# Two decoder layers written out without loop or barrier, the first eight expert blocks fixed by the program, a loop for second blocks alone

## The chip, the cores and the metric

The kernel runs on one core of one Trainium2 chip. The metric is the device time of one execution in microseconds, the median of several runs. The core has five instruction streams that run side by side and meet only at semaphores: PE (TensorE, matmuls and transposes), DVE (VectorE), ACT (ScalarE), POOL (GpSimd) and SP (SyncE, which issues the DMAs).

## The reference, cut to what matters

```python
for i in range(DEPTH):                     # DEPTH = 2, 256 tokens, D_MODEL = 1024, float32
    h = rms_norm(x, mix_norm_g[i])
    proj = h @ w_in[i]                     # SSD, gMLP, attention and gate columns
    ...                                    # three branches
    merged = g_ssd * (y_ssd @ w_br_ssd[i]) + g_sgu * (y_sgu @ w_br_sgu[i]) + g_mla * (y_mla @ w_br_mla[i])
    x = x + merged @ w_out[i]
    h = rms_norm(x, ffn_norm_g[i])
    if i % 2 == 0: x = x + swiglu(h, ...)          # dense, 2816 wide
    else:          x = x + moe_ffn(h, ...)         # 8 experts, 3584 wide, top 2 of 8
```

`moe_ffn` weighs each expert's output by a softmax over the token's two largest router logits; an expert that a token did not choose has weight zero for it.

## The kernel before, in words

**Exact products.** Every large weight panel (512 columns, 2 MB) comes in by DMA and is cut into four pieces of 128x1024. ACT copies a piece to a rounded "high" part (`w_hi`, in the mixer `mixer_hi`), DVE subtracts to get the "low" part (`w_lo`), and PE does three matmuls for each product: high by high, low by high, high by low. PE waits for each piece on `lo_made`. `w_hi` has six slots (`HI_SLOTS`), DVE and ACT work up to four pieces ahead (`AHEAD`).

**Two layers in one loop.** Each engine runs `Fori(0, DEPTH)`: the mixer (branches, `out` projection), then the norm and transposes of the feed-forward part, then, under `If(L < 1)`, the dense feed-forward. At the end of an iteration each of PE, ACT and DVE adds one to `arrived`; POOL waits for three, fills the padding of the convolution with zeros, clears the semaphores and adds one to `go`, on which all start again through `begin`. This is the barrier of the text below.

**The router and the items.** After layer 1 and its barrier, PE computes the logits (L1113), DVE chooses two experts for each token, and PE ranks the tokens of each expert (to L1122). DVE then builds a table of items (L1992 to L2026): an item is one block of at most 128 tokens of one expert, so there are eight items, and one more for each expert with over 128 tokens (at most 11 in all, `MAX_ITEMS`). The number of items goes to `item_tab` and signals `routed`.

**The items.** PE gathers an item's tokens with a one-hot `pick` matrix (L1130), DVE and ACT make `xg_hi` and `xg_lo`. A barrier follows. The item is 21 panels (gate, up and down of seven column ranges). At its first up panel PE scatters the output of the item before (L1142, from `ysb` by way of `wpickT`) and DVE adds it to `x` (L2051); for the first item this output is zeros (L2057). At its last up panel PE gathers the next item's tokens. Items 0 to 6 (`STRAIGHT` = 7) are written out. The rest are a loop `Fori(STRAIGHT, n_items)` with a barrier ahead of each iteration. After the loop comes one more barrier, the scatter of the last item and the output DMA (L713). SP's own loop over items is `Fori(0, n_items)`; it reads the expert's number from `item_tab` and keeps a ring of seven slots (`MOE_RING`) filled ahead of use, over the end of an item too.

Of the kernel before, what the change touches and what calls it, by code (L numbers as in the profile page):

```python
# [12 lines left out]
P = 128  # L30
# [205 lines left out]
STRAIGHT = EXPERTS - 1  # L236
assert len(MOE.pieces) % HI_SLOTS == 0 and EARLY <= MOE.first[1]
SCATTER_BANKS = (6, 7, 1, 3)

# [19 lines left out]
def hybrid_trunk(nc, A, out):  # L259
    with ExitStack() as ctx:  # L260
# [180 lines left out]
        ring_full = [sem(f"ring_full{s}") for s in range(MOE_RING)]  # L441
        ring_used = [sem(f"ring_used{s}") for s in range(MOE_RING)]
# [5 lines left out]
        fills_begun = sem("fills_begun")  # L448
        routed = sem("routed")
        finished = sem("finished")  # L450

# [4 lines left out]
        def local(name):  # L456
# [3 lines left out]

        bank_full = local("bank_full")
        bank_free = [local(f"bank_free{b}") for b in range(8)]
        act_steps = local("act_steps")
# [8 lines left out]
            "kpe_made", "kv_copied", "gated", "hsq_made", "hmean_made", "hroot_made", "hnorm_made", "max_made",  # L472
# [4 lines left out]
            "picked", "gathered", "xg_made", "xg_hi_made", "xg_lo_made", "wpickT_full", "wpickT_made",  # L477
            "y_copied", "scattered", "added", "zeroed",
            "logits", "chosen", "ranks", "gap_made", "gap_exp",
            "zeros_made")}  # L480
# [5 lines left out]
        splitters = {}  # L486

# [11 lines left out]
        def piece_free(eng, c):  # L499

            if c >= MIXER_HI_SLOTS:
                what, n = USED[c - MIXER_HI_SLOTS]
                if what == "job":
                    eng.wait_ge(bank_full, JOB[n] + 1)
                else:
                    eng.wait_ge(S["mixer_piece_used"], n)
# [15 lines left out]
        def take(eng, name):  # L522

            keep_ahead(eng, name)
            eng.wait_ge(bank_full, JOB[name] + 1)
            return ps[:, JOB[name] % 8]
# [5 lines left out]
        def given(eng, name):  # L532

            keep_ahead(eng, name)
            eng.wait_ge(bank_free[JOB[name] % 8], JOB[name] // 8 + 1)

        def wait_panel(eng, split, kind, i, past=0):

            eng.wait_ge(S["panel_done"], past * len(split.order) + split.at[(kind, i)] + 1)
# [14 lines left out]
        def hidden_free(eng, split, i, tiles, past=0):  # L554

            if i > 2 - tiles:
                wait_panel(eng, split, "down", i - (1 if tiles == 2 else 2), past)
# [7 lines left out]
        def hi_free(eng, split, c, past=0):  # L565

            c += past * len(split.pieces)
            if c >= HI_SLOTS:
# [3 lines left out]
                if last:  # L572
                    eng.wait_ge(S["panel_done"], u + 1)
                else:
                    eng.wait_ge(S["piece_used"], c - HI_SLOTS + 1 - u)
# [5 lines left out]
        def begin(eng, turn):  # L581

            eng.wait_ge(go, turn)
            eng.sem_inc(begun, 1)
# [25 lines left out]
        def _(sp):  # L610
# [4 lines left out]
            with sp.Fori(0, DEPTH) as L:  # L615
                one = bass.ds(L, 1)

                def panel(use):
# [5 lines left out]
                    if c == 0:  # L624

                        sp.sem_inc(fills_begun, 1)
# [11 lines left out]
                sp.sem_inc(fills_begun, 1)  # L638
# [14 lines left out]
                sp.wait_ge(go, L + 1)  # L653
# [7 lines left out]
                with sp.If(L < 1):  # L661
# [17 lines left out]
            def moe_panel(item, u, expert):  # L679
                kind, p = MOE.order[u]  # L680
                c, width = MOE_PANELS[p]
                s, n = u % MOE_RING, u // MOE_RING

                sp.wait_ge(ring_used[s], item * ITEM_USES + (uses0[s] + n + 1))
# [9 lines left out]
            for u in range(RING):  # L694
                moe_panel(0, u, slice(0, 1))

            sp.wait_ge(go, DEPTH + 1)
            for u in range(RING, MOE_RING):
                moe_panel(0, u, slice(0, 1))
# [3 lines left out]
            with sp.Fori(0, n_items) as i:  # L703
                e = sp.value_load(item_tab[0:1, bass.ds(i, 1)], min_val=0, max_val=EXPERTS - 1)
                for u in range(MOE_RING, len(MOE.order)):
                    moe_panel(i, u, bass.ds(e, 1))
                with sp.If(i < n_items - 1):
                    e2 = sp.value_load(item_tab[0:1, bass.ds(i + 1, 1)], min_val=0, max_val=EXPERTS - 1)
                    for u in range(MOE_RING):
                        moe_panel(i + 1, u, bass.ds(e2, 1))  # L710
# [7 lines left out]
        def _(pool):  # L718
# [8 lines left out]
            pool.sem_inc(go, 1)  # L727
            with pool.Fori(0, DEPTH):
                pool.wait_ge(arrived, 3)

                pool.memset(xin[:, :, :, 0:TAPS - 1], 0.0).then_inc(S["zeros_made"], 1)
                pool.wait_ge(S["zeros_made"], 1)
                pool.sem_clear(cleared)
                pool.sem_inc(go, 1)
            pool.wait_ge(arrived, 3)
            n_items = pool.value_load(item_tab[0:1, ITEM_SLOTS:ITEM_SLOTS + 1], min_val=EXPERTS, max_val=MAX_ITEMS)
            pool.sem_clear(cleared)  # L737
            pool.sem_inc(go, 1)
            pool.wait_ge(arrived, 3)
            pool.sem_clear(cleared)  # L740
            pool.sem_inc(go, STRAIGHT)
            with pool.Fori(STRAIGHT, n_items):
# [6 lines left out]
        def _(pe):  # L749
# [3 lines left out]
            def bank(name):  # L753
# [4 lines left out]
                if i >= 8:  # L758
                    pe.wait_ge(bank_free[i % 8], i // 8)
# [30 lines left out]
            def ffn(split, tiles, slot_of, lhs, acc, before_turn=None, before_down=None, early=0, past=0):  # L790
# [4 lines left out]
                panels_past, pieces_past = past * len(split.order), past * len(split.pieces)  # L795

                def turn_hidden(i):
                    pe.wait_ge(S["h_made"], past * n_panels + i + 1)
# [5 lines left out]
                for c, (u, at_, n, ends) in enumerate(split.pieces):  # L804
                    kind, i = split.order[u]
                    s, width = slot_of(u), split.widths[i]
                    if kind == "up" and i and at_ == 0:
                        pe.wait_ge(S["hid_made"], past * n_panels + i)
                    if kind == "down" and at_ == 0:
                        pe.wait_ge(S["hid_made"], past * n_panels + i + 1)  # L810
                    if pieces_past + c >= early:
                        pe.wait_ge(S["lo_made"], pieces_past + c + 1 - early)
# [23 lines left out]
                    if ends:  # L836
                        unreleased.append((s, S["panel_done"], panels_past + u + 1))
# [13 lines left out]
            with pe.Fori(0, DEPTH) as L:  # L851
# [15 lines left out]
                def split_piece():  # L867
# [3 lines left out]
                    pe.wait_ge(S["mixer_lo_made"], c + 1)  # L871
                    return mixer_piece(c)[2:]

                def project(name, lhs):
# [19 lines left out]
                    unreleased.append((s, bank_full, turn[0]))  # L894

                def close_part(br, i, y, ready):
# [8 lines left out]
                    if i == 2:  # L905
                        pe.wait_ge(S["yT_lo_made"], 4 * ("ssd", "sgu", "mla").index(br) + 4)
# [3 lines left out]
                begin(pe, L + 1)  # L910
# [3 lines left out]
                for t in range(NT):  # L914
                    pe.wait_ge(S["normed"], t + 1)
                    for hh in range(2):
                        turn_over(f"ht{t}{hh}", [xn[:, t, c * P:(c + 1) * P] for c in range(4 * hh, 4 * hh + 4)])
                pe.wait_ge(S["h_lo_made"], 4)

                for n in range(3):  # L920
# [14 lines left out]
                    unreleased.append((s, bank_full, turn[0]))  # L935
# [4 lines left out]
                pe.wait_ge(S["adt_made"], 1)  # L940
# [8 lines left out]
                pe.wait_ge(S["silu_made"], 6)  # L949
# [12 lines left out]
                for t in range(NT):  # L962
                    pe.wait_ge(S["lat_normed"], t + 1)
# [11 lines left out]
                unreleased.append((s, bank_full, turn[0]))  # L975
# [7 lines left out]
                unreleased.append((s, bank_full, turn[0]))  # L983
                project("u1", hsplit)

                pe.wait_ge(S["xd_made"], 1)
# [6 lines left out]
                for c in range(NT):  # L993
# [10 lines left out]
                    pe.wait_ge(S["xs_made"], c + 1)  # L1004
                    for g in range(2):
                        pe.wait_ge(S["mt_made"], 4 * c + 2 * g + 2)
# [19 lines left out]
                pe.wait_ge(bank_full, turn[0])  # L1026
                pe.sem_inc(vec_used, 1)
                for i in range(5):
                    close_part("ssd", i, xh, lambda t: pe.wait_ge(S["y_normed"], t + 1))
# [1127 lines left out]
```

## Time and profile before

| | |
|---|---|
| time, median of 3 runs | 2103.87 us |
| lowest, highest | 2099.33, 2107.67 us |
| span of the profiled execution | 2098.5 us |
| time of the profiled execution itself | not given apart; the three runs are the times |
| PE, DVE, ACT busy | 94%, 73%, 60% of the span |
| PE's clock, mean granted | 0.968 |
| read from HBM | 495.22 MB, 236 GB/s over the span |

The span runs from the first to the last instruction of the profiled execution. The shares of busy time are means over stages with different limits. The two layers take the first half of the span and the items the second.

### The profile page before, as it was taken

How to read it: one execution, taken by the hardware profiler on the slowest of the kernel's cores; microseconds unless marked ns; L12 is line 12 of the kernel's file. 1: busy time of each engine (PE TensorE's matmuls, PEld its weight loads, DVE VectorE, ACT ScalarE, POOL GpSimd, SP SyncE). 2: the span in 40 equal slices, each digit the busy share in tenths (PEclk: the TensorE clock that was granted, in tenths of full speed). 3: DMA queues.
4: the chain of work that ended last, by engine and by line, in shares of the span. 5: the costliest groups of instructions: out<-in, count | busy, mean ns of one | idle time of the engine just before them, and what ended most of it. 6: DMA issues, size and time to landing. Idle time of an engine off the chain costs nothing.

```text
span 2098.5 us, 24842 instructions
## 1 busy us (share of the span) xinstructions
PE 1964.5 (94%) x9464; PEld 1626.9 (78%) x9464; DVE 1533.4 (73%) x1915; ACT 1264.9 (60%) x1593; POOL 1.3 (0%) x10
## 2 busy tenths in 40 slices
PE   6898999889988898999759999999999999999998
PEld 6687877768878687887648888888888888888787
DVE  6677565554438667474459899899898989889897
ACT  4665464343435655554327777677777767777675
POOL 0000000000000000000000000000000000000000
PEclk9999998989998999998969999999999999999999
DMA  6343432435544433333459999899999999999891
GB/s 223 119 149 133 148 121 81 162 129 191 181 147 155 156 123 121 121 121 121 148 213 350 358 339 378 325 374 348 346 373 332 372 342 361 344 352 376 306 377 75
DMA packets 220045, 497.92 MB, mean 237 GB/s; under 512 B 8631, under 2 KB 14997, under 8 KB 219669
## 3 DMA queue, kind: packets, MB, share of 16 engines
q1 hardware_dynamic: 219924, 496.29, 66.1%
q8 instruction: 79, 1.29, 0.3%
q14 instruction: 42, 0.34, 0.0%
HBM read 495.22 MB, written 1.05 MB: 236 GB/s over the span
## 4 chain that ended last, share of the span: by engine, by line
PE 87%; DVE 6%; ACT 3%; issue 2%; DMA 1%; PEldq 0%; SPq 0%; POOLq 0%; DVEq 0%; POOL 0%; ACTq 0%
PE ps L830 12%; PE ps L832 12%; PE ps L831 12%; PE ps L885 7%; PE ps L886 6%; PE ps L887 6%; PE ps L821 6%; PE ps L823 6%; PE ps L822 6%; PE ps L1130 2%; PE ps L1142 1%; PE ps L801 1%; PE ps L778 1%; PE ps L930 1%; PE ps L928 1%
## 5 line engine op out<-in xcount | busy, mean ns | idle before, releaser
L1522 DVE TENSOR_TENSOR w_lo<-piece,w_hi 128x1024 fp32r<-128x1024 f32 (+1 forms) x742 | 855.4, 1214 | 103.5 <-ACT w_hi L1189 103.3
L1189 ACT ACTIVATE w_hi<-piece 128x1024 fp32r<-128x1024 f32 (+1 forms) x742 | 731.7, 1048 | 89.8 <-PE ps L823 37.8
L830 PE MATMUL ps<-w_hi,xg_hi 128*128 128x512 f32 x896 | 354.3, 395 | 7.5 <-POOLq L737 5.6
L832 PE MATMUL ps<-w_hi,xg_lo 128*128 128x512 f32 x896 | 349.6, 390 | 0.0
L1582 DVE TENSOR_TENSOR w_lo<-piece,mixer_hi 128x1024 fp32r<-128x1024 f32 (+1 forms) x192 | 229.3, 1216 | 164.7 <-ACT mixer_hi L1238 164.5
L831 PE MATMUL ps<-w_lo,xg_hi 128*128 128x512 f32 x896 | 349.2, 390 | 0.0
L1238 ACT ACTIVATE mixer_hi<-piece 128x1024 fp32r<-128x1024 f32 (+1 forms) x192 | 197.9, 1049 | 198.8 <-PE ps L887 165.6
L821 PE MATMUL ps<-w_hi,hid_hi 128*128 128x512 f32 x536 | 209.4, 391 | 1.5 <-DVE hid_lo L1557 1.5
L823 PE MATMUL ps<-w_hi,hid_lo 128*128 128x512 f32 x536 | 208.8, 390 | 0.0
L822 PE MATMUL ps<-w_lo,hid_hi 128*128 128x512 f32 x536 | 208.6, 389 | 0.0
L830 PEld LDWEIGHTS ps<-w_hi,xg_hi 128*128 128x128 f32 x896 | 168.7, 188 | 41.4 <-issue 8.0
L832 PEld LDWEIGHTS ps<-w_hi,xg_lo 128*128 128x128 f32 x896 | 168.5, 188 | 35.9
L831 PEld LDWEIGHTS ps<-w_lo,xg_hi 128*128 128x128 f32 x896 | 168.8, 188 | 33.6
L885 PE MATMUL ps<-mixer_hi,hT_hi 128*128 128x512 f32 (+1 forms) x416 | 166.9, 401 | 6.9 <-DVE w_lo L1582 6.2
L886 PE MATMUL ps<-w_lo,hT_hi 128*128 128x512 f32 (+1 forms) x416 | 164.4, 395 | 0.0
L887 PE MATMUL ps<-mixer_hi,hT_lo 128*128 128x512 f32 (+1 forms) x416 | 163.7, 393 | 0.0
L1213 ACT ACTIVATE hid_hi<-ps 128x512 fp32r<-128x512 f32 (+1 forms) x62 | 39.3, 634 | 202.3 <-PE ps L801 202.3
L821 PEld LDWEIGHTS ps<-w_hi,hid_hi 128*128 128x128 f32 x536 | 100.7, 188 | 22.3 <-DVE hid_lo L1557 1.7
L823 PEld LDWEIGHTS ps<-w_hi,hid_lo 128*128 128x128 f32 x536 | 100.6, 188 | 21.0
L822 PEld LDWEIGHTS ps<-w_lo,hid_hi 128*128 128x128 f32 x536 | 100.6, 188 | 20.6
L1557 DVE TENSOR_TENSOR hid_lo<-ps,hid_hi 128x512 fp32r<-128x512 f32 (+1 forms) x62 | 45.5, 734 | 81.9 <-ACT hid_hi L1213 81.9
L887 PE MATMUL ps<-mixer_hi,yT_lo 128*128 128x512 f32 x256 | 103.5, 404 | 0.0
(275 smaller groups left out, 2594.5 us busy)
## 6 DMA issues: line engine op xcount, KB each, us to landing
piece<-in_moe_w_gate SPq DMA_DIRECT2D x56, 2048.0 KB, 8.6
piece<-in_moe_w_up SPq DMA_DIRECT2D x56, 2048.0 KB, 8.9
piece<-in_moe_w_down SPq DMA_DIRECT2D x56, 2048.0 KB, 8.5
piece<-in_w_in SPq DMA_DIRECT2D x30, 2048.0 KB, 8.9
piece<-in_ffn_w_gate SPq DMA_DIRECT2D x5, 2048.0 KB, 7.8
piece<-in_ffn_w_up SPq DMA_DIRECT2D x5, 2048.0 KB, 8.0
piece<-in_ffn_w_down SPq DMA_DIRECT2D x5, 2048.0 KB, 7.8
piece<-in_w_br_ssd SPq DMA_DIRECT2D x4, 2048.0 KB, 8.5
```

The costliest lines, as they stand in the source:

```text
L821: pe.matmul(acc(t, half), a_hi, hi[:, cs_], start=start, stop=False)
L822: pe.matmul(acc(t, half), a_hi, lo[:, cs_], start=False, stop=False)
L823: last = pe.matmul(acc(t, half), a_lo, hi[:, cs_], start=False, stop=stop)
L830: pe.matmul(b, a_hi, hi[:, cs_], start=(kk == 0), stop=False)
L831: pe.matmul(b, a_hi, lo[:, cs_], start=False, stop=False)
L832: last = pe.matmul(b, a_lo, hi[:, cs_], start=False, stop=(kk == KD - 1))
L885: pe.matmul(b, a_hi, hi[:, j, :], start=(kk == 0), stop=False)
L886: pe.matmul(b, a_hi, lo[:, j, :], start=False, stop=False)
L887: last = pe.matmul(b, a_lo, hi[:, j, :], start=False, stop=(kk == KD - 1))
L1189: act.activation(hi, slots[s][:, at_:at_ + n], ACT.Copy).then_inc(S["hi_made"], 1)
L1522: dve.tensor_tensor(w_lo[s][:, at_:at_ + n], slots[s][:, at_:at_ + n], hi.bitcast(F32), ALU.subtract).then_inc(S["lo_made"], 1)
L1582: dve.tensor_tensor(lo, value, hi.bitcast(F32), ALU.subtract).then_inc(S["mixer_lo_made"], 1)
```

## The change

The loop over layers becomes Python code that runs when the program is built, so both layers stand in each engine's program, and semaphore targets grow with the layer (`passed`, `job_done`) where they were cleared before. The barriers after layer 0, after layer 1, ahead of item 0 and ahead of item 7 go. Layer 1 starts when `x_made` says that DVE has added the dense output.

The first eight items are experts 0 to 7, in that order, for every routing. Expert 0 no longer scatters zeros, expert 7 no longer gathers a next item. The table of items now holds only second blocks (`second_blocks`), and DVE builds it inside expert 0, behind its second column range, in place of ahead of item 0.

Second blocks are a loop `Fori(EXPERTS, n_items)` on every engine, behind a barrier. One iteration is a block on its own: SP reads the expert's number and loads the panels, PE gathers, multiplies and scatters, DVE adds to `x`. `n_items` is still eight and one for each expert with over 128 tokens.

```diff
-            with sp.Fori(0, DEPTH) as L:
+            for L in range(DEPTH):
...
-                sp.wait_ge(go, L + 1)
+                if L:
+                    sp.wait_ge(x_made, 4 * L)
...
+            for e in range(EXPERTS):
+                for u in range(len(MOE.order)):
+                    if e == 0 and u == RING:
+                        sp.wait_ge(bank_full, (DEPTH - 1) * len(JOBS) + JOB["out11"] + 1)
+                    s, n = u % MOE_RING, u // MOE_RING
+                    sp.wait_ge(ring_used[s], e * ITEM_USES + uses0[s] + n + 1)
+                    moe_panel(u, slice(e, e + 1))
...
-            with sp.Fori(0, n_items) as i:
+            with sp.Fori(EXPERTS, n_items) as item:
+                begin(sp, item)
+                e = sp.value_load(item_tab[0:1, bass.ds(item, 1)], min_val=0, max_val=EXPERTS - 1)
+                for u in range(len(MOE.order)):
+                    s, n = u % MOE_RING, u // MOE_RING
+                    if n:
+                        sp.wait_ge(ring_used[s], n)
+                    moe_panel(u, bass.ds(e, 1))
+                sp.wait_ge(block_added, item - (EXPERTS - 1))
+                sp.sem_inc(begun, 1)
...
-            with pe.Fori(0, DEPTH) as L:
+            for L in range(DEPTH):
...
-                begin(pe, L + 1)
...
-                with pe.If(L < 1):
+                if L < 1:
...
+            for e in range(EXPERTS):
+                expert_block(e, DENSE_ADDS, e > 0, e < EXPERTS - 1)
+            release()
+            scatter(EXPERTS - 1)
...
-            with pe.Fori(STRAIGHT, n_items) as item:
-                begin(pe, item + (DEPTH + 2))
-                expert_block(0)
+            with pe.Fori(EXPERTS, n_items) as item:
+                begin(pe, item)
+                gather(1)
+                expert_block(0, NOTHING, False, False)
                 release()
+                scatter(0)
+                pe.wait_ge(S["scattered"], 4)
                 pe.sem_inc(arrived, 1)
...
                 for t in range(NT):
+                    if L:
+                        act.wait_ge(x_made, 4 * L - 4 + 2 * t + 2)
                     act.activation(vs[:, t, :], x[:, t, :], ACT.Square, accum_out=ss[:, t:t + 1]).then_inc(S["squared"], 1)
...
+                def after(i):
+                    if i == 0 and e:
+                        add_outputs(S["added"], e - 1)
+                    if i == 1 and not e:
+                        second_blocks()
...
+            copy_y(EXPERTS - 1, DENSE_ADDS)
+            add_outputs(finished, EXPERTS - 1)
```

On PE, at the end of the program, the rows ahead of and at the head of the loop over items, of the kernel before (L1172 is the loop, L830 to L832 are the matmuls of a gate panel):

```order
L823 MATMUL ps<-w_hi,hid_lo 128x512
L1172 UNCONDITIONAL_BRANCH
L1172 ISA
L830 MATMUL ps<-w_hi,xg_hi 128x512
L831 MATMUL ps<-w_lo_97,xg_hi 128x512
```

and its tail:

```order
L1172 REGISTER_ALU
L1172 COMPARE_AND_BRANCH
L583 REGISTER_ALU
L1142 MATMUL ps<-piece_89,piece_92 128x512 x4
L260 UNCONDITIONAL_BRANCH
```

The same head in the changed kernel (L1144 is the scatter, L1133 the gather, L1177 the loop, L836 and on a gate panel):

```order
L1144 MATMUL ps<-piece_89,piece_92 128x512 x4
L1176 TENSOR_LOAD item_tab
L1176 ISA x2
L1177 UNCONDITIONAL_BRANCH
L1177 ISA
L1133 MATMUL ps<-piece_90,piece_85 128x128 x16
L836 MATMUL ps<-w_hi,xg_hi 128x512
```

and its tail:

```order
L829 MATMUL ps<-w_hi,hid_lo 128x512
L1144 MATMUL ps<-piece_89,piece_92 128x512 x4
L1177 REGISTER_ALU
L1177 COMPARE_AND_BRANCH
L261 UNCONDITIONAL_BRANCH
```

The scatter of the last expert moved ahead of the loop, and the loop has a gather and a scatter of its own. In both programs the compare stands behind the body. For contrast, the `If(L < 1)` of the kernel before, L1102, has its compare ahead of the dense panels:

```order
L778 MATMUL ps<-const,piece_85 128x128 x16
L1102 COMPARE_AND_BRANCH
L830 MATMUL ps<-w_hi,hT_hi 128x512
```

On SP the changed loop has the same form: behind the last panel of expert 7, a load of `n_items`, the unconditional branch, a load of the expert's number, and the panels:

```order
L700 DMA piece_55<-in_moe_w_down 128x4x1024
L713 TENSOR_LOAD item_tab
L713 ISA x2
L714 UNCONDITIONAL_BRANCH
L714 ISA
L716 ISA
L716 TENSOR_LOAD item_tab
L716 ISA x2
L700 ISA
L700 DMA piece_49<-in_moe_w_gate 128x8x512
```

Before, SP's loop followed the seventh panel of item 0; it now follows the last panel of expert 7.

## Rows read from the trace of the kernel before

**Rows 1.** The page: DMA issues of one weight, KB each, us to landing.
```profile
piece<-in_moe_w_gate SPq DMA_DIRECT2D x56, 2048.0 KB, 8.6
```

**Rows 2.** Chain that ended last, its scatters: start us, us, what.
```profile
1099.68 3.43 PE ps L1142 x8
...
1848.48 3.43 PE ps L1142 x8
...
1975.40 3.43 PE ps L1142 x8
```

**Rows 3.** Timeline at the end of layer 0: start us, us, engine, line.
```profile
623.70 2.48 DVE L1944 TENSOR_TENSOR x<-ps,x 128x512 f32<-128x512 f32 x4 [5.83 <-PE ps L823]
627.14 1.28 ACT L1243 ACT_TABLE_LOAD   x1 [8.54 <-POOLq L733]
630.43 0.19 ACT L1243 ACTIVATION_READ_ACCUMULATOR piece<-x 128x1 f32 x1
632.79 0.20 ACT L1245 ACTIVATE small<-small 128x2 f32<-128x2 f32 x1 [0.88 <-DVE small L1566]
634.04 3.68 PE L778 MATMUL ps<-const,piece 128*128 128x128 f32 x16 [4.64 <-DVE piece L1596]
```

**Rows 4.** Chain, from the end of layer 1 to the logits.
```profile
1047.32 7.01 PEldq L1102
...
1055.31 0.78 PE ps L1113 x3
```

**Rows 5.** Timeline of DVE from the ranks to item 0.
```profile
1067.61 0.17 DVE L1992 TENSOR_SCALAR piece<-ps 128x16 f32<-128x16 f32 x1 [1.20 <-PE ps L1122]
1068.24 0.17 DVE L1997 TENSOR_SCALAR piece<-ps 128x8 f32<-128x8 f32 x1
1075.34 0.46 DVE L2030 TENSOR_SCALAR piece<-const,piece 128x128 f32<-128x128 f32 x2
1083.49 1.23 DVE L2043 TENSOR_TENSOR xg_lo<-piece,xg_hi 128x1024 fp32r<-128x1024 f32 x1 [1.19 <-ACT xg_hi L1462]
```

**Rows 6.** Windows: PE, PEld, DVE, ACT, POOL busy, PEclk, DMA share, GB/s.
```profile
1059.00:1062.40 3.40, 3.28 (x16) 3.18 (x15) 2.01 (x3) 0.18 (x1) 0.00 (x0) 0.50 1.06 405
1087.00:1089.00 2.00, 1.83 (x4) 1.49 (x5) 0.97 (x2) 1.85 (x3) 0.00 (x0) 0.50 0.00 0
1225.00:1350.00 125.00, 125.00 (x576) 102.71 (x575) 111.92 (x111) 91.55 (x101) 0.00 (x0) 1.00 0.97 354
```

**Rows 7.** Timeline of PE and DVE in item 0: start, scatter, first turn.
```profile
1087.17 0.77 PE L830 MATMUL ps<-w_hi,xg_hi 128*128 128x512 f32 x1 [5.59 <-POOLq L737]
1099.52 3.59 PE L1142 MATMUL ps<-piece,piece 128*128 128x512 f32 x8
1100.41 0.68 DVE L1550 TENSOR_TENSOR piece<-ps,piece 128x512 f32<-128x512 f32 x1
1102.95 0.60 PE L801 MATMUL ps<-const,piece 128*128 128x128 f32 x4
```

**Rows 8.** Timeline of a steady column range in item 0.
```profile
1136.93 0.48 PE L830 MATMUL ps<-w_hi,xg_hi 128*128 128x512 f32 x1
1137.91 0.69 DVE L1557 TENSOR_TENSOR hid_lo<-ps,hid_hi 128x512 fp32r<-128x512 f32 x1 [0.67 <-ACT hid_hi L1213]
```

**Rows 9.** Timeline from the last gather but one to item 7's start.
```profile
1947.12 3.73 PE L1130 MATMUL ps<-piece,piece 128*128 128x128 f32 x32
1950.90 0.60 PE L801 MATMUL ps<-const,piece 128*128 128x128 f32 x4
1964.27 0.47 PE L830 MATMUL ps<-w_hi,xg_hi 128*128 128x512 f32 x1 [1.86 <-POOLq L741]
```

**Rows 10.** Timeline of the end.
```profile
2088.93 0.39 PE L823 MATMUL ps<-w_hi,hid_lo 128*128 128x512 f32 x1
2091.02 3.70 PE L1142 MATMUL ps<-piece,piece 128*128 128x512 f32 x8 [1.70 <-DVE piece L2071]
2094.76 0.69 DVE L2051 TENSOR_TENSOR x<-ps,x 128x512 f32<-128x512 f32 x1 [0.17 <-PE ps L1142]
```

More of the change, by code:

```diff
@@ L1151, in gather_next, with expert_block, before_down @@
                 last.then_inc(S["wpickT_full"], 1)
-            gather(1)
-            pe.wait_ge(S["gathered"], 2)
+            def expert_block(past, before, scatters, gathers):
+                def before_down():
+                    if scatters:
+                        pe.wait_ge(S["added"], 2 * past)
+                    if gathers:
+                        gather(past + 2)
+                    turn_weights(past)
+                pe.wait_ge(S["xg_lo_made"], past + 1)
+                ffn(MOE, 1, moe_slot, lambda kk, t: (xg_hi[:, kk, :], xg_lo[:, kk, :]), lambda t, half: ps[:, 4 + half],
+                    before, (lambda: scatter(past - 1)) if scatters else None, before_down, past)
+            gather(1)
+            for e in range(EXPERTS):
+                expert_block(e, DENSE_ADDS, e > 0, e < EXPERTS - 1)
+            release()
+            scatter(EXPERTS - 1)
+            pe.wait_ge(S["scattered"], 4 * EXPERTS)
             pe.sem_inc(arrived, 1)
@@ L1220, in _ @@
             act.wait_ge(setup_done, 4)
-            with act.Fori(0, DEPTH) as L:
-                begin(act, L + 1)
+            for L in range(DEPTH):
+                layer[id(act)] = L
                 leads = [0]
@@ L1438, in _ @@
                         act.activation(hT_hi[cut], hT[cut], ACT.Copy).then_inc(S["hT_hi_made"], 1)
[L1439 to L1444 removed]
+                    ffn(DENSE, NT, dense_slot, dense_full, NOTHING)
             def lead_early(past):
@@ L1569, in _ @@
             dve.wait_ge(setup_done, 4)
-            with dve.Fori(0, DEPTH) as L:
-                chain.n = 0
-                begin(dve, L + 1)
+            for L in range(DEPTH):
+                layer[id(dve)] = L
                 rests = [0]
@@ L1943, in _ @@
                             cut = x[:, t, half * N:(half + 1) * N]
-                            dve.tensor_tensor(cut, ps[:, 4 + 2 * t + half], cut, ALU.add)
-                assert chain.n == steps
-                link(dve.tensor_copy(small[:, 509:510], small[:, 510:511]))
-                dve.sem_inc(arrived, 1)
-            chain.n = 0
-            begin(dve, DEPTH + 1)
+                            dve.tensor_tensor(cut, ps[:, 4 + 2 * t + half], cut, ALU.add).then_inc(x_made, 1)
             rest_early(0)
@@ L1998, in _ @@
-            link(dve.tensor_copy(start, cst("expert", E8)))
-            for e in range(1, E8):
-                link(dve.tensor_tensor(start[:, e:E8], start[:, e:E8], big[:, e - 1:e].to_broadcast([P, E8 - e]), ALU.add))
-            grid = [by(items[:, n, :], h=E8) for n in range(8)]
-            number = by(cst("item", ITEM_SLOTS * E8), h=E8)
-            which = by(cst("expert", ITEM_SLOTS * E8), h=E8)
-            expert_of = items[:, 4, 0:ITEM_SLOTS]
-            block_of = items[:, 5, 0:ITEM_SLOTS]
@@ L2092, in _, with after_more @@
-            begin(dve, DEPTH + 2)
-            for it in range(STRAIGHT):
-                expert_block(slice(it, it + 1), slice(it + 1, it + 2), it)
-                rest_early((it + 1) * len(MOE.pieces) - EARLY)
-            dve.wait_ge(S["xg_lo_made"], STRAIGHT)
-            dve.wait_ge(S["panel_done"], STRAIGHT * len(MOE.order))
-            dve.sem_inc(arrived, 1)
-            with dve.Fori(STRAIGHT, n_items) as item:
-                begin(dve, item + (DEPTH + 2))
-                expert_block(bass.ds(item, 1), bass.ds(item + 1, 1), 0)
-                with dve.If(item < n_items - 1):
-                    rest_early(len(MOE.pieces) - EARLY)
-                dve.wait_ge(S["xg_lo_made"], 1)
-                dve.wait_ge(S["panel_done"], len(MOE.order))
+            with dve.Fori(EXPERTS, n_items) as item:
+                begin(dve, item)
+                pos, weight = more_block_of(item)
+                pick_tokens(pos)
+                take_tokens(0)
+                rest_of_tokens(0)
+                def after_more(i):
+                    if i == len(MOE_PANELS) - 3:
+                        weigh_tokens(pos, weight)
+                ffn(MOE, 1, moe_slot, NOTHING, after_more)
+                copy_y(0, NOTHING)
+                add_outputs(S["added"], 0)
+                dve.wait_ge(S["added"], 2)
+                dve.sem_inc(block_added, 1)
```

550 lines of the change are left out of this document (265 added, 285 removed).

## The prediction

> **What bounds the kernel now.** I read the page first. Each expert weight has 56 DMA issues [rows 1]; an item has seven gate panels, so exactly eight items run on these inputs, and no expert has over 128 tokens. Then the chain that ended last: through the items it is PE, and the scatters of items 0 and 6 are 748.8 us apart, 124.8 us an item, while the next period, over the barrier ahead of item 7, is 126.92 us [rows 2]. A window over one item shows PE busy for all 125 us at the full clock, DVE for 112, and the DMA queues at 97% with 354 GB/s [rows 6]. So an item is bound by PE, with DMA close behind; nothing in the change makes an item itself shorter, apart from its gather and scatter. What can be gained lies in the gaps between stages, which I read from the timelines: after layer 0 [rows 3], after layer 1 [rows 4], from the ranks to item 0 [rows 5, 7], and at the end [rows 9, 10].
>
> **The part that decides: what the loop does with eight items.** The changed loop runs from 8 while below `n_items`, and `n_items` is 8 here. Read as a Python range it has no iteration. The program's rows say otherwise: ahead of the body stands only an unconditional branch to it, the one compare stands behind the body, on PE and on SP alike; where a construct may be skipped (`If`), the compare stands ahead. So the body runs once before anything is compared. The loop before had the same form, but started at 7, where one iteration was due. I expect a ninth item: expert 0 read from a table of zeros, positions of -128 that pick no token, weights zero, 21 panels of 2 MB loaded and multiplied for nothing. The output stays right, which is why it can go unseen.
>
> **The gaps closed, each against the span of 2098.5 us.**
>
> After layer 0: DVE's four adds end at 626.18, PE's transposes begin at 634.04 [rows 3]. Before, the two squares waited for the barrier and a table load (627.14 to 628.42) and ended at 630.62, 1.10 us each. After, the first square runs beside the last adds. The second starts at 626.2 and ends at 627.3, a table load for the square root takes 1.28 us again, and from the root's start to PE it was 1.25 us (632.79 to 634.04): PE at 629.9, **4.2 us** earlier.
>
> After layer 1: PE's queue is at L1102, the `If` that skips the dense panels, for 7.01 us, and the logits start at 1055.31 after POOL's barrier [rows 4]. Written out, neither is there: from 1047.32 that is **8.0 us**. The Trainium skill (Advanced Engine Details and Errata, Control Flow Timing) gives about 108 ns for a compare-and-branch; by it this term would be 1.1 us and the end 6.9 us later. The row has the duration of this very branch, so the sum takes the row. The logits ran at a granted clock of 0.50 [rows 6], the lower of the two levels. They will now follow transposes at once, where before there was a gap, so some may run at the higher level: between 0 and 3.5 us (half of their 7), I take **1.5**.
>
> Routing: from the ranks (1067.61) DVE works through the table until 1075.34 [rows 5]. After, only two small operations of 0.21 us pitch precede the pick: 7.3 us, less 0.1 for a table load that now stands ahead of the small exponential and lies mostly beside the ranks: **7.2 us**.
>
> Ahead of item 0: `xg_lo` ends at 1084.72 [rows 5], the first matmul is at 1087.17 [rows 7]: 2.45 us of barrier and value loads, of which 0.1 stays: **2.35 us**. That start had four matmuls in 2 us at clock 0.50 [rows 6], where steady ones take about 0.23 us each; the loss was up to 1.3 us. With the shorter gap it may go or stay: **0.7**.
>
> Item 0 without its scatter: PE gets 3.43 us back [rows 2], but the scatter hid the wait for `h`: DVE's multiplication starts 0.9 us after the up panel and takes 0.68 [rows 7], so 1.6 us now show. Gain **1.8 us**.
>
> `second_blocks` inside item 0: the table's 30 operations took 7.1 us (1068.24 to 1075.34) [rows 5]; the new 27 I put at 6.9. They start when `hid_lo` of the second range is done, 1.67 us after the next gate panel starts [rows 8]. PE has four pieces in hand, 5.5 us (eight pieces and a slow start took 12.35 us [rows 7], 1.37 a piece without it). The next low part comes at 1.67 + 6.9 + 1.2, so PE stands **4.3 us**. The bounds are 0, if DVE were further ahead, and 6.9. ACT, with six slots, goes on meanwhile.
>
> Item 7: no barrier ahead, 126.92 - 124.8 = **2.1 us**. No gather: its up panel to the turn took 3.78 us [rows 9], now 1.6 for `h` again: **2.2 us**. At the end PE stopped at 2089.32 and scattered at 2091.02 [rows 10]; a copy of 0.7 us and two signals make 0.8: **0.9 us**.
>
> Together 4.2 + 9.5 + 7.2 + 3.05 + 1.8 - 4.3 + 2.1 + 2.2 + 0.9 = **26.7 us**. The eight experts' last add, before at 2095.45, ends at 2068.8.
>
> **The ninth item.** Nothing overlaps its start: SP waits for `go`, so its ring is empty, where items so far found seven panels loaded. Barrier about 0.96 us (626.18 to 627.14 [rows 3]), a value load 0.75 (half of 2.45 - 0.96, two in a row there), the first 2 MB panel 8.6 us [rows 1], copy and subtraction of a piece 2.1 (about 1 us each by the busy times and counts of [rows 6]): first matmul at 2068.8 + 12.4 = 2081.2. The tokens are ready by then: pick to `xg_lo` took 9.4 us [rows 5]. PE's work: item 7 took 125.05 us (1964.27 to 2089.32); without scatter and gather, but with both waits for `h`, 125.05 - 3.43 - 3.78 + 3.2 = 121.0, plus 1.3 for a start at the low clock. That ends at 2203.5. Supply: 2.097 MB at 354 to 405 GB/s [rows 6] is 5.2 to 5.9 us a panel against PE's 5.8, so DMA follows or costs 2 us at worst. Copy, scatter and adds 5.2 us (0.8, and 2091.02 to 2095.45), then the two outputs together, 3.7 us where they took 3.05 with the first sent early: the span ends at 2212.4.
>
> That is 113.9 us more than 2098.5. The profiled execution has no time of its own here; the median is 5.4 us above its span, the runs 0.8 to 9.2. I carry the 5.4 over: **2218 us**, 5.4% slower.
>
> **Rivals.**
>
> *The loop is skipped.* If the branch at the head did test, or the count were below, the experts would end at 2068.8 and the outputs 3.05 us later. PE would jump over the body after its scatter (2068.1), and if that costs the 7.01 us of [rows 4] it ends at 2075. Time 2075 + 5.4 = 2080, 1.1% faster. The Trainium skill (Runtime: NRT & Kernel Launch, Instruction fetch mechanics) says that a taken branch beyond the fetched pages stalls while code is loaded; by it alone the end would wait for PE in this case, and the 7.01 us row agrees. It decides wholly at one point: body run or not. Against it speak the rows of the program and the eight items of [rows 1]. Chance 0.03.
>
> *The ninth item costs more than an item.* If DMA from an empty ring lands at the low rate and its first panels late (11 us rather than 8.6), and DVE falls behind PE without the four early pieces, 5 to 10 us are added: 2223 to 2228. The window with DVE busy 112 of 125 [rows 6] leaves it room, so 0.17.
>
> *The gaps give back little.* If PE's 7.01 us is time for code that has to be loaded in straight order too, and second blocks stall PE by the full 6.9, some 10 us of the 26.7 are lost: 2228. Chance 0.10; it would show as PEldq or issue in the chain near the logits.
>
> *More found than counted.* Logits and first matmuls wholly at the high clock, no stall from second blocks: 7 us less, 2211. Chance 0.10.
>
> My forecast, 2213 to 2223, has 0.60. With the neighbours the range is 2206 to 2231. Change within 0.5% (11 us, about what this kernel's runs, 8 us apart, can tell) needs the ninth item to be hidden, for which I see nothing: 0.01. Faster 0.03, slower 0.96.
>
> **What the new profile would show.** Each expert weight with 63 DMA issues and 44 MB more read (539 MB); a hole of 12 to 17 us on PE near 2065 with the low clock behind it, then a full item without gather and scatter inside. PE's logits some 12 us earlier than before, no 7 us in its queue, one wait of about 4 us for a low part in item 0. Wrong would be 56 issues (skipped), or the hole absent. A shift in the gaps moves the result by a few us; only the loop moves it across the 0.5%.

## The result, and the profile after

The changed kernel takes 2221.57 us, median of 4 runs (2217.92 to 2229.29); the kernel before took 2105.77 us in the same session (4 runs, 2099.33 to 2110.02). The ratio is 1.055, 95% interval 1.053 to 1.058: 5.5% slower. Forecast were 2218 us and a range of 2206 to 2231.

The page of the changed kernel, its head, its bytes and the DMA issues of one expert weight:

```profile
span 2227.5 us, 25493 instructions
...
PE 2096.7 (94%) x9998; PEld 1733.9 (78%) x9998; DVE 1637.9 (74%) x2007; ACT 1352.2 (61%) x1688; POOL 1.2 (0%) x9
...
HBM read 539.26 MB, written 1.05 MB: 243 GB/s over the span
...
piece<-in_moe_w_gate SPq DMA_DIRECT2D x63, 2048.0 KB, 8.3
```

There are 63 issues where [rows 1] had 56, and 44 MB more are read: 21 panels of 2 MB. A ninth item runs.

The gaps that answer to [rows 3 to 7], from the timeline of the changed kernel (start us, us, engine, line; in brackets the idle time ahead and what ended it; rows picked out):

```profile
627.86 2.48 DVE L1944 TENSOR_TENSOR x<-ps,x 128x512 f32<-128x512 f32 x4 [5.87 <-PE ps L829]
...
631.54 1.28 ACT L1252 ACT_TABLE_LOAD   x1
...
634.08 1.33 PE L784 MATMUL ps<-const,piece 128*128 128x128 f32 x5 [5.81 <-DVE piece L1595]
...
1044.62 3.67 PE L784 MATMUL ps<-const,piece 128*128 128x128 f32 x16 [4.53 <-DVE piece L1927]
1049.38 6.97 PE L1116 MATMUL ps<-r_w,hT 128*128 128x8 f32 x32 [1.08 <-DVE hT L1931]
...
1061.60 0.17 DVE L1986 SCALAR_TENSOR_TENSOR piece<-ps,chosen 128x16 f32<-128x16 f32 x1 [1.20 <-PE ps L1125]
1062.02 0.48 DVE L1998 TENSOR_SCALAR piece<-const,piece 128x128 f32<-128x128 f32 x2
1062.56 6.15 PE L1133 MATMUL ps<-piece,piece 128*128 128x128 f32 x32 [1.06 <-DVE piece L1998]
1070.56 1.22 DVE L2016 TENSOR_TENSOR xg_lo<-piece,xg_hi 128x1024 fp32r<-128x1024 f32 x1 [1.12 <-ACT xg_hi L1464]
1071.84 0.79 PE L836 MATMUL ps<-w_hi,xg_hi 128*128 128x512 f32 x1 [3.13 <-DVE xg_lo L2016]
```

From the end of the adds of layer 0 (630.34) to PE it is 3.74 us, before 7.86. The logits start 0.35 us behind `hT`, without the branch that held PE's queue for 7 us. From the ranks to the pick it is 0.42 us, before 7.73. From `xg_lo` (1071.78) to the first matmul it is 0.06 us, before 2.45. From the transposes behind layer 1 to the first matmul of item 0 it is 27.22 us; before, 44.35.

The waits of PE in item 0, and windows over the logits, the start of item 0, the stretch behind the 3.9 us wait, and the start and body of the ninth item (the columns are those of [rows 6]):

```profile
engine line waited for: us in total, times, longest us
PE ps L836 <- DVE w_lo L1523: 3.9, 1, 3.9
PE ps L836 <- DVE xg_lo L2016: 3.1, 1, 3.1
PE ps L808 <- DVE piece L1550: 1.5, 1, 1.5
```

```profile
1049.40:1056.30 6.90, 6.90 (x32) 6.86 (x32) 4.16 (x4) 0.00 (x0) 0.00 (x0) 0.50 1.05 386
1072.00:1077.00 5.00, 5.00 (x12) 3.94 (x13) 3.16 (x3) 1.48 (x2) 0.00 (x0) 0.50 0.46 168
1115.00:1118.50 3.50, 3.50 (x10) 2.81 (x9) 3.50 (x4) 1.11 (x2) 0.00 (x0) 0.53 0.89 295
2094.20:2098.00 3.80, 3.80 (x9) 3.03 (x10) 3.21 (x3) 2.28 (x3) 0.00 (x0) 0.50 1.05 387
2100.00:2200.00 100.00, 98.32 (x445) 81.10 (x445) 89.29 (x85) 75.39 (x84) 0.00 (x0) 1.00 1.00 378
```

The logits stayed at the lower level. The start of item 0 ran at it for over 5 us, before for less than 3. The stall behind `second_blocks` has a stretch at that level behind it as well.

The end of the eight experts and the start of the ninth item, then its last add and the outputs (rows picked out):

```profile
2079.67 0.69 DVE L2029 TENSOR_TENSOR x<-ps,x 128x512 f32<-128x512 f32 x1 [0.17 <-PE ps L1144]
2081.80 0.48 DVE L1998 TENSOR_SCALAR piece<-const,piece 128x128 f32<-128x128 f32 x2 [1.44 <-POOLq L750]
2081.96 0.40 SPq L700 DMA_DIRECT2D piece<-in_moe_w_gate  x1
2091.69 3.90 ACT L1194 ACTIVATE w_hi<-piece 128x1024 fp32r<-128x1024 f32 x4 [3.69 <-DMA piece<-in_moe_w_gate]
2094.15 0.77 PE L836 MATMUL ps<-w_hi,xg_hi 128*128 128x512 f32 x1 [7.97 <-DVE w_lo L1523]
...
2222.03 0.69 DVE L2029 TENSOR_TENSOR x<-ps,x 128x512 f32<-128x512 f32 x1 [0.17 <-PE ps L1144]
2223.07 0.84 SPq L726 DMA_DIRECT2D out<-x  x2
```

Eight experts are done at 2080.36. One more item, whose tokens are all zeros, takes until 2222.72: 142.4 us. The signs that the forecast had named are there: 63 issues, 539 MB, no row of 7 us for PE's queue, one wait of about 4 us for a low part in item 0. The logits start 5.9 us earlier than before, not the forecast 12; the late layers of this execution hide the rest.

### The profile page after: what moved, and what is told of

Same layout as the page of the kernel before. It is cut to its first block, busy times and chain, and to the rows that moved or that the text cites. A ratio compares the mean times of both kernels' runs of the same rounds, so it can differ in the third digit from the quotient of the medians.

```text
span 2227.5 us, 25493 instructions
## 1 busy us (share of the span) xinstructions
PE 2096.7 (94%) x9998; PEld 1733.9 (78%) x9998; DVE 1637.9 (74%) x2007; ACT 1352.2 (61%) x1688; POOL 1.2 (0%) x9
## 4 chain that ended last, share of the span: by engine, by line
PE 88%; DVE 6%; ACT 3%; issue 2%; DMA 1%; SPq 0%; POOL 0%; POOLq 0%; DVEq 0%; ACTq 0%
PE ps L836 12%; PE ps L838 12%; PE ps L837 12%; PE ps L892 6%; PE ps L893 6%; PE ps L894 6%; PE ps L829 6%; PE ps L827 6%; PE ps L828 6%; PE ps L808 2%; PE ps L1144 1%; PE ps L1133 1%; PE ps L784 1%; PE ps L936 1%; PE ps L934 1%
## 5 line engine op out<-in xcount | busy, mean ns | idle before, releaser
L1523 DVE TENSOR_TENSOR w_lo<-piece,w_hi 128x1024 fp32r<-128x1024 f32 x826 | 952.5, 1214 | 107.6 <-ACT w_hi L1194 107.6
L1194 ACT ACTIVATE w_hi<-piece 128x1024 fp32r<-128x1024 f32 x826 | 814.8, 1048 | 95.4 <-PE ps L838 42.6
L836 PE MATMUL ps<-w_hi,xg_hi 128*128 128x512 f32 x1008 | 400.8, 398 | 15.0 <-DVE w_lo L1523 11.8
L838 PE MATMUL ps<-w_hi,xg_lo 128*128 128x512 f32 x1008 | 395.2, 392 | 0.0
L837 PE MATMUL ps<-w_lo,xg_hi 128*128 128x512 f32 x1008 | 394.6, 391 | 0.0
L827 PE MATMUL ps<-w_hi,hid_hi 128*128 128x512 f32 x592 | 231.3, 391 | 1.5 <-DVE hid_lo L1557 1.5
L836 PEld LDWEIGHTS ps<-w_hi,xg_hi 128*128 128x128 f32 x1008 | 190.9, 189 | 53.6 <-issue 12.4
L829 PE MATMUL ps<-w_hi,hid_lo 128*128 128x512 f32 x592 | 230.6, 389 | 0.0
L838 PEld LDWEIGHTS ps<-w_hi,xg_lo 128*128 128x128 f32 x1008 | 190.5, 189 | 40.9
L837 PEld LDWEIGHTS ps<-w_lo,xg_hi 128*128 128x128 f32 x1008 | 191.1, 190 | 38.4
```

The source lines that it names most:

```text
L827: pe.matmul(acc(t, half), a_hi, hi[:, cs_], start=start, stop=False)
L829: last = pe.matmul(acc(t, half), a_lo, hi[:, cs_], start=False, stop=stop)
L836: pe.matmul(b, a_hi, hi[:, cs_], start=(kk == 0), stop=False)
L837: pe.matmul(b, a_hi, lo[:, cs_], start=False, stop=False)
L838: last = pe.matmul(b, a_lo, hi[:, cs_], start=False, stop=(kk == KD - 1))
L1194: act.activation(hi, slots[s][:, at_:at_ + n], ACT.Copy).then_inc(S["hi_made"], 1)
```

## The experiments

The theory is that the ninth item is the whole loss and that the gaps give some 20 to 27 us back. Its rivals are that straight code costs what the barriers did, or that something other than an item takes the time. In the second group the question was what takes away part of the gain.

**1. No loop.** The loop over second blocks is left out on all engines (here PE):

```diff
-            pe.wait_ge(S["scattered"], 4 * EXPERTS)
-            pe.sem_inc(arrived, 1)
-            pe.wait_ge(routed, 1)
-            n_items = pe.value_load(item_tab[0:1, ITEM_SLOTS:ITEM_SLOTS + 1], min_val=EXPERTS, max_val=MAX_ITEMS)
-            with pe.Fori(EXPERTS, n_items) as item:
-                ...
```

> The changed kernel with the loop over second blocks taken out on all five engines, with its handshake and value loads (second blocks are left out; these inputs have none). My theory: a ninth item, run for nothing, is all that makes the changed kernel slower. Its last add of eight experts was at 2080.4; outputs take 3.1 to 3.7 us more and about 1.8 lie outside the span: 2078 to 2086 us, 0.9 to 1.3% faster than before, each expert weight with 56 DMA issues. Rival 'straight code costs as much as the barriers': 2100 to 2110, no change from before. Rival 'all 26.7 us of the gaps come, the 8 us missing in the profile are the clock of one execution': 2074 to 2078.

Measured: 2079.46 us (4 runs, 2072.33 to 2081.89), ratio to before 0.9865 (0.9843 to 0.9887), with 56 issues. The changed kernel without its ninth item is 1.3% faster than before. Its item 0, in the timeline of PE:

```profile
1066.22 0.79 PE L816 MATMUL ps<-w_hi,xg_hi 128*128 128x512 f32 x1 [3.13 <-DVE xg_lo L1964]
...
1081.57 0.66 PE L788 MATMUL ps<-const,piece 128*128 128x128 f32 x4 [1.47 <-DVE piece L1498]
...
1108.38 0.47 PE L816 MATMUL ps<-w_hi,xg_hi 128*128 128x512 f32 x1 [3.86 <-DVE w_lo L1471]
```

From 1066.22 to the last add (2074.76) it is 1008.54 us; in the changed kernel 1008.52. The execution differs, the stretch does not.

**2. The loop inside an `If`.** On every engine:

```diff
-            with pe.Fori(EXPERTS, n_items) as item:
-                ...
+            with pe.If(n_items > EXPERTS):
+                with pe.Fori(EXPERTS, n_items) as item:
+                    ...
```

> The changed kernel with its loop inside an If (count of items above eight) on all five engines, so that the compare stands ahead of the body. Theory: the body is skipped and the time is that of the kernel without the loop, plus what the jump over the body costs on PE. That starts behind the last scatter and handshake; with the 7.01 us that PE's queue stood in the If over the dense panels it would end 2 to 4 us behind the outputs: 0 to 4 us over the kernel without the loop. Rival: a jump costs 0.1 us, no difference. If the If does not keep the body from running: 2221.

Measured: 2083.19 us (5 runs, 2074.05 to 2087.20), ratio 0.990 (0.988 to 0.992). The body is skipped, and the code for second blocks is still there; the inputs of all runs here have none, so no run shows it at work. The last rows of the timeline of DVE and the page's span, first of this kernel, then of the one without the loop:

```profile
span 2072.2 us, 23968 instructions
...
2066.30 0.69 DVE L2033 TENSOR_TENSOR x<-ps,x 128x512 f32<-128x512 f32 x1 [0.17 <-PE ps L1146]
```

```profile
span 2077.8 us, 23942 instructions
...
2074.07 0.69 DVE L1977 TENSOR_TENSOR x<-ps,x 128x512 f32<-128x512 f32 x1 [0.17 <-PE ps L1124]
```

Behind the last add it is 5.21 us, against 3.04 us: what is left of the loop costs 2.2 us at the end (in the kernel of experiment 7, which has the same loop in an `If`, it is 5.37 us behind the last add). The kernel without the loop also lacks the handshake and the load of the count, so the 2.2 us belong to these and the jump together. That the jump on PE is what takes them fits the 7.01 us of [rows 4], started behind PE's last scatter, but the profile shows no row for it here, nor which engine ends last; that is argued, not shown. The Trainium skill (Advanced Engine Details and Errata, Control Flow Timing) gives about 108 ns for a compare-and-branch; by it alone both kernels would end about 3.04 us behind the last add. The 2.2 us more do not fit that, and the branch that has a row of its own, the 7.01 us of [rows 4], speaks against it for a jump over a body of this size.

**3. One more item in the kernel before, and in the changed kernel.** The same edit in both:

```diff
-            link(dve.tensor_scalar(items[:, 6, 0:1], items[:, 6, 0:1], float(EXPERTS), None, ALU.add))
+            link(dve.tensor_scalar(items[:, 6, 0:1], items[:, 6, 0:1], float(EXPERTS + 1), None, ALU.add))
```

> The kernel before with the count of items raised by one: a ninth item, expert 0 without tokens, runs in the old loop, with its seven early panels loaded during item 7 and its gather and scatter inside. Theory: it costs one period over the barrier, 126.9 us: 2232 us, ratio 1.060. The changed kernel's ninth took 142.4 us from the last add of item 7 to its own. Rival 'an item without work is cheaper, since it has no tokens': under 120 us. Rival 'a ninth item costs more whatever stands ahead of it': 142 us.

> The changed kernel with the count of items raised by one, to nine. Theory: the body runs before anything is compared, so with a count of nine it runs once, as with eight: time and DMA issues (63 of each expert weight) do not change, 2221 us, ratio to before 1.055. Rival 'the loop tests first and something else runs or waits 125 us in the changed kernel': a further item, 2345 to 2365.

Measured: the kernel before takes 2232.01 us with nine items (2227.11 to 2233.93, ratio 1.059, 1.057 to 1.061). The changed kernel takes 2223.82 us with a count of nine (2219.93 to 2227.48, ratio 1.056), and 2221.57 with eight, with the same 63 issues. Counts of eight and nine give the same run: the body is executed before anything is compared. In the kernel before, the chain has the scatters of its last two iterations at

```profile
1980.16 3.43 PE ps L1142 x8
...
2108.84 3.43 PE ps L1142 x8
```

so a ninth item costs 128.7 us there, although it has no tokens either. In the changed kernel it costs 142.4.

**4. A count of ten in the changed kernel.**

> The changed kernel with the count of items raised to ten: the loop body runs for items 8 and 9, both without tokens. Theory: what makes the ninth cost 142 us instead of the 124.8 of an item is its start with an empty ring and its end that nothing overlaps, and that comes with each iteration: 2 x 142 over the kernel without the loop, about 2364 us, first matmul of each body 12 to 15 us behind the last add ahead of it. Rival 'only the entry into the loop is dear (its code comes from memory once)': the second iteration costs 130 us or less, 2352.

Measured in one run: 2362.92 us, with 70 issues. The last adds of the eight experts and of the two iterations:

```profile
2073.19 0.69 DVE L2029 TENSOR_TENSOR x<-ps,x 128x512 f32<-128x512 f32 x1 [0.17 <-PE ps L1144]
...
2215.09 0.69 DVE L2029 TENSOR_TENSOR x<-ps,x 128x512 f32<-128x512 f32 x1 [0.17 <-PE ps L1144]
...
2355.72 0.69 DVE L2029 TENSOR_TENSOR x<-ps,x 128x512 f32<-128x512 f32 x1 [0.17 <-PE ps L1144]
```

That is 141.9 and 140.6 us: the price comes with each iteration, and entering the loop adds 1.3 us at most in this run. An item on its own costs 16 to 18 us more than the 124.8 of one in the row: the first matmul comes 13.3 and 12.1 us behind the last add.

**5. What the table costs in item 0.** From the kernel without the loop, the 27 operations of `second_blocks` are left out, or handed out in portions:

```diff
-                    if i == 1 and not e:
-                        second_blocks()
+                    if not e and i < 4:
+                        some_of_table(5)
+                    if not e and i == 5:
+                        some_of_table(20)
```

> The kernel without the loop, and without the 27 operations that make the table of second blocks (it leaves out second blocks wholly; these inputs have none). In the kernel without the loop PE stands 3.86 us for a low part behind these operations, and some eight matmuls behind the wait have a pitch of 0.43 us instead of 0.23. Theory: both come from them: 3.9 + 1.6 = 5.5 us less than the kernel without the loop, about 2074 us, first matmul of item 0 to its end 5.5 us shorter. Rival 'the low clock has another cause': 3.9 us. Rival 'another wait takes its place, since DVE is behind from the start of the item': 0 to 2 us.

> The kernel without the loop, with the 27 operations in portions of five behind panels 0 to 3 of item 0 and the rest behind panel 5. DVE stands 2 to 3 us per panel there, a portion takes 1.3 us. Theory: the work was never the price, its being in one piece was: the same 5.5 us less as with no such operations, about 2074 us, no wait of PE over 1 us for a low part in item 0. Rival 'DVE has no room so early in item 0, since it works off the start': small waits add up and 2 us or less come back, 2077 us.

Measured: 2076.66 us without the table (6 runs, 2063.11 to 2077.71, ratio 0.985, 0.981 to 0.988) and 2077.27 with portions (6 runs, 2074.69 to 2084.55, ratio 0.987, 0.985 to 0.990). Whole times can't tell these apart from 2079.46, which was taken in another session; single executions of one kernel differ by up to 18 us (experiment 6). The stretch can: from the first matmul of item 0 to the last add it is 1002.77 us in both, 5.77 less than 1008.54. The waits of PE in item 0, with portions:

```profile
PE ps L816 <- DVE xg_lo L1964: 3.1, 1, 3.1
PE ps L788 <- DVE piece L1498: 1.5, 1, 1.5
```

The wait for a low part is gone and nothing has taken its place. So 3.86 us of it were the wait and the other 1.9 us are for the most part the matmuls at half clock behind it, and the work itself is free when it comes in pieces.

**6. The clock at the start of item 0.** In the kernel without the loop:

```diff
             gather(1)
+            pe.wait_ge(S["hi_made"], DENSE_ADDS["hi_made"] + 1)
+            for _ in range(7):
+                pe.matmul(ps[:, 4], w_hi[:, 0, 0:P], w_hi[:, 0, 0:N], start=True, stop=True)
             for e in range(EXPERTS):
```

> The kernel without the loop, with seven matmuls of 128x512 more behind the first gather, into a bank that is free then: PE works through most of the 3.13 us in which it waits for the low part of the first tokens. Theory: the 13 matmuls of item 0 at half clock follow PE's idle time ahead of them, a term that I had counted as a gain of 0.7 us and that came out as a loss: fewer of them run slow, 1.3 to 2.7 us less from the first matmul to the turn (15.35 us there). Rival 'the clock there has nothing to do with that wait': the stretch stays at 15.35 us and the whole is the same, or 0.5 us longer where the additional matmuls end too late. The difference is near what the times can tell, so the stretch in the profile decides.

Measured: 2077.45 us (6 runs, 2069.29 to 2087.19, ratio 0.987, 0.984 to 0.990); again the stretch decides. From the first matmul to the turn it is 12.62 us (1058.51 to 1071.13), against 15.35. Windows over the gap ahead of the first matmul and over the matmuls behind it, first without the additional matmuls, then with them:

```profile
1063.00:1066.00 3.00, 0.09 (x1) 0.00 (x0) 1.75 (x2) 2.15 (x3) 0.00 (x0) 0.86 1.06 390
1066.30:1071.50 5.20, 5.20 (x12) 4.05 (x13) 3.36 (x3) 1.56 (x2) 0.00 (x0) 0.50 0.46 169
```

```profile
1055.40:1058.40 3.00, 1.60 (x7) 0.95 (x6) 1.86 (x3) 2.26 (x3) 0.00 (x0) 1.00 1.05 386
1058.60:1063.60 5.00, 5.00 (x22) 4.15 (x23) 4.31 (x4) 3.59 (x4) 0.00 (x0) 1.00 0.91 335
```

The clock was up at the end of the gather and fell near the end of the 3.13 us in which PE stood (0.86 over that gap: 1.00 up to 1065.0, 0.50 from 1065.5); the first 12 or 13 matmuls paid for it. With an idle time of 1.51 us it did not fall, here and in the profile of experiment 7. The cost of that wait is 2.7 us on top of its own length.

**7. All of it together.** The guarded kernel with portions and with the seven matmuls.

> The guarded kernel (all parts of the computation there) with the table in portions and the seven additional matmuls. Theory: 2083.2 - 5.5 - 2 = about 2076 us, ratio to before 0.985; the jump over the body on PE keeps the end 2.2 us behind that of the same kernel without a loop. Rival 'gains do not add up, DMA takes over in item 0, with its first panels only just there': 2079 to 2083.

Measured: 2075.39 us (6 runs, 2073.05 to 2083.78), ratio to before 0.986, interval 0.983 to 0.989: 1.4% faster than before, 6.6% below the changed kernel's time of the first session, and with nothing of the computation left out. From the first matmul of item 0 to the last add it is 1000.09 us: 1008.54 - 5.77 - 2.73 would be 1000.04. The gains add up. Against the guarded kernel alone the stretch is 8.4 us shorter (1008.51 there), and the medians differ by 7.8, with wide intervals.

**8. The kernel before, twice more.**

> The kernel before, unchanged, for one more profile. Question: the shown profile of before has a span of 2098.5 us, its runs a median of 2106. Theory: executions differ in where stretches of the two layers run at the lower clock, and nowhere else; the transposes behind layer 1 begin anywhere from 1040 to 1052 us, and from the first matmul of item 0 to the last add it is 1008.3 us again. Rival: the difference lies in the items.

> The kernel before once more, for the spread: as in the run ahead of this one. If the layers written out gave more than the 4.1 us of the gap between them, the transposes behind layer 1 of the kernel before would begin more than 4 us later on average than the 1039.1 us that eight profiles of the kernels with written-out layers show on average (1031.4 to 1044.6).

Measured, in one run each: 2109.38 and 2111.72 us, with spans of 2107.4 and 2109.8 us, where the profile shown before has 2098.5. Rows of the chain in the second of them (the scatters inside items 5, 6 and 7):

```profile
1733.31 3.43 PE ps L1142 x8
...
1858.11 3.43 PE ps L1142 x8
...
1986.65 3.43 PE ps L1142 x8
```

The period over the barrier ahead of item 7 is 128.54 us here, and so it is in the other two further profiles of this loop; in [rows 2] it is 126.92. The shown profile was a lucky execution: its barrier, its start of item 0 and its layers were each at the good end. The theory of that expectation, that only the layers differ, fell: the items differ by 2 to 3 us too.

With all profiles the account of the kernel without the loop closes:

| stretch | kernel before | layers written out | gain |
|---|---|---|---|
| to the transposes behind layer 1 | 1042.8 to 1050.3, mean of 4 1046.5 | 1031.4 to 1044.6, mean of 9 1039.0 | 7.5 |
| transposes to first matmul of item 0 | 44.0 to 46.0, mean of 4 45.1 | 27.2 (7 profiles) | 17.9 |
| first matmul to last add of eight items | 1008.3 to 1011.4, mean of 3 1010.0 | 1008.5 | 1.5 |

The sum is 26.9 us; the medians (2106.2 and 2079.46) differ by 26.7. The forecast's gaps gave 26.7 as well, but in these three rows as 4.2, 19.05 and 3.4: the sum agrees, the terms do not, and that it agrees is luck.

## Why the prediction was right, and where its terms were off

The step that decides held: the body runs once with a count of eight. Without it the kernel is 1.3% faster, with it 5.5% slower, and the counts of nine and ten show the same from the other side. The rival "the loop is skipped" gave 2080 us; the kernel without it and the one that skips it take 2079.5 and 2083.2. The pieces that follow are read from the profile of the changed kernel, whose span is 15.1 us above the forecast 2212.4:

- **After layer 0** (4.2): 4.1 by the gap, right. But the transposes behind layer 1 came at 1044.62 where 1038.6 follows from the forecast: 6.0 us. Nine profiles with the same code ahead of this place spread over 13 us; this was the latest. That is the spread of executions, not the change.
- **After layer 1** (8.0, and 1.5 for the clock): 8.0 came, as the branch's own row said. The 1.5 did not: all 32 logit matmuls ran at 0.50 in seven profiles. In the profiles of experiments 6 and 7 they took 4.9 and 4.5 us instead of 6.97, with the same code up to there, so it is a matter of the execution.
- **Routing** (7.2): 7.3, but the gather took 0.4 us longer.
- **Ahead of item 0** (2.35 and 0.7): 2.4 by the gap. The 0.7 has the wrong sign: the stretch at half clock grew. The step was "With the shorter gap it may go or stay". It can grow too. In the shown profile of before the clock was back 2.7 us after the first matmul, in the changed kernel after 5.7; why it comes back sooner or later was not tried. From the first matmul to the scatter of item 0 the three further profiles of the old loop take 13.0 to 14.0 us where [rows 2, 7] give 12.5, so the shown one had the short stretch.
- **Item 0 without its scatter** (1.8): the waits for `h` are 1.46 and 1.24 us, forecast 1.6. With the clock of the start, the stretch to the turn gained 0.4 us instead of 2.5.
- **Second blocks** (-4.3): the wait is 3.86, with what it does to the clock 5.77. This is the mis-sized term: a stall of PE was priced at its own length.
- **Item 7** (2.1 and 2.2) and **the end** (0.9): every period is 124.80 us; the wait for `h` 1.24; scatter at 0.80 us behind the last matmul, as forecast. From item 0's first matmul to the last add the terms gave 1004.9, measured were 1008.5: 2.1 of the 3.6 us are the start of item 0, 1.5 the stall.
- **The ninth item**: first matmul 13.8 us behind the last add, forecast 12.4 (first panel 9.7 us from issue to ACT, taken as 8.6). PE then took 123.35, forecast 122.3. Copy, scatter and adds 5.22, forecast 5.2. Outputs 4.8 instead of 3.7.
- **The 5.4 us carried over** as median above span: a wrong reading that came out well. Time less span is 1.8 to 2.2 us in every run here; the rest was that the shown execution was a fast one.

Together: 6.0 + 1.9 + 3.6 + 1.4 + 1.1 + 0 + 1.1 = 15.1 us above the forecast span. The carried 5.4 was 3.6 too much, and the profiled execution was 7.7 us slower than the median: 2217.8 + 15.1 - 3.6 - 7.7 = 2221.6. The 3.6 us in the items come back in every profile of this code, the 6.0 in the layers do not. The terms behind the layers were 9.1 us short together, and the figure carried over was 3.6 too large: that the forecast lies within 4 us of the median is in part luck.

Of the rivals, "the ninth item costs more" came true in part (2.5 us, not 5 to 10), and DVE did keep up. "The gaps give back little" did not: the chain of the changed kernel has no row of PE's queue at all, where the kernel before has 7.01 us of it, so PE waited for no code in straight order. The 7.5 us of the table's first row are over the mark of 4 us that the last expectation had set for a gain of the layers themselves. Split at the end of layer 0, the means of the same four and nine profiles are: the adds of layer 0 end at 628.2 and 625.7 us, from there to PE it is 8.0 and 3.7 us, and from PE to the transposes behind layer 1 410.4 and 409.6 us. So 4.3 us are the gap, as forecast; 2.5 us lie in layer 0 and 0.8 in layer 1, where single profiles with the same code differ by 6 and 10 us (layer 0) and by 4 and 6 (layer 1). Whether the layers gained these 3 us by losing the loop stays open.

## What to carry to other kernels

Ask of every loop with a bound from data what it does when it has no iteration to run, and read the answer from where the compare stands, not from the source; the output does not show the extra pass, only the time and the counts of DMA issues, bytes and instructions do. Price a stall of PE by its own length and by the stretch at the lower clock behind it, here 3.9 + 1.9 and 3.1 + 2.7 us, and hand out work of a helper engine in small pieces (here five operations behind a panel instead of 27). And take more than one profile of the kernel before when the terms are a few microseconds: here one execution lay 6 us below the median in three different places.

## What the runs showed of the hardware

- Within an idle time of 3.13 us ahead of item 0 the granted clock fell from 1.00 (0.86 over the gap) and some 13 matmuls ran at the lower of its two levels, 1.2 GHz; with 1.51 us idle it stayed up (seven profiles and two). The stretch does not follow from the idle time alone: in the kernel before PE stood 5.59 us at this place in all four profiles, and 6 to 13 matmuls ran slow. Seven matmuls into an unused bank, 1.87 us of work, were worth 2.73 us.
- Behind the wait of 3.86 us in item 0 the first five matmuls still had a pitch of 0.23 to 0.31 us and the fall came only then (0.42 to 0.43 us for the next seven): here the stall's cost in clock lay wholly behind it, where ahead of item 0 the clock fell within the idle time.
- The barrier ahead of item 7 cost 2.1 us in one profile and 3.7 in three others, with the same code up to there.
- A loop on all engines that is skipped by an `If`, with the load of its count and its handshake, costs 2.2 us at the end of the program (5.21 and 5.37 us behind the last add in two profiles, 3.04 to 3.12 in four without it).
- The branch over the dense panels, taken once, held PE's queue for 7.01 us in [rows 4] and for 6.71 to 7.30 us in three further profiles of the old loop.
